# A hybrid decoder layer on one core: the input projection by seven block products a pair of column tiles instead of eight

## The chip, the cores and the metric

The kernel runs on one core of one Trainium2 chip. The metric is the device time of one execution in microseconds, the median of several runs. The engines are named as in the profile: PE is TensorE (matrix multiplication), PEld its weight loads, DVE is VectorE, ACT is ScalarE, POOL is GpSimd, and SP is the engine that issues almost all DMA transfers. Each engine works through its own list of instructions strictly in order. Where an instruction has to wait for a semaphore, everything behind it on that engine waits too.

## The reference

One layer of a causal decoder over 1024 tokens of width 1024, all in float32:

```
xn   = rms_norm(x, norm1_w)
proj = xn @ w_in            # 1024 x 6408: q, k, v (768 each), conv q/k/v (1536), beta and a (8), z (512), 2 gates (1024 each)
o_a  = three groups of 4 heads, causal windows (128,1), (512,4), (2048,16), softmax, combined by their log-denominators
o_b  = gated delta rule in chunks of 64 on silu(conv(dqkv)), 4 heads of 128, rms_norm, times silu(z)
y    = sigmoid(gate_a) * (o_a @ w_pa) + sigmoid(gate_b) * (o_b @ w_pb)
h    = x + y @ w_o
out  = rms_norm(h + (silu(conv gate) * conv val) @ w_down, final_norm_w)   # conv(rms_norm(h) @ w_up), d_ff 2816
```

To keep float32 accuracy, the kernel writes every operand of a matrix product as a high part (rounded to the type fp32r) and a low part (the rest), and adds three products: high by high, high by low and low by high.

## The kernel before, in words

**Stages.** A head normalises x, transposes it and splits it into `xh` and `xl` (8 tiles of K by 1024 tokens each). The mixer computes the input projection and, between its matmuls, the delta rule and attention. `merge_and_project` computes the branch projections, the gates and the output projection. `ffn` follows. Its up projection already uses seven block products in place of eight (class `UpRoom`).

**The input projection before.** It is 51 jobs: one of 16 columns (`ba`), then 50 of 128 columns: 12 `conv`, 4 `z`, 18 `q`, `k`, `v` and 16 `gate`. A job of 128 columns is 8 steps of K, and each step (an item `mm`, which calls `product3`) is 6 matmuls 128x512: three products by two halves of the tokens. So a job is 48 matmuls into one of the two accumulators `acc`. Its weights arrive as one 512 KB load (`w_raw`). ACT makes the high part (L1085) and POOL the low part (L1007). At the end of the job ACT empties the accumulator (`evac`).

**What sets the order.** `mixer_schedule` writes one list of items by hand. Every engine's function (`x_sync`, `x_gpsimd`, `x_scalar`, `x_vector`, `x_tensor`) walks the same list and emits its own part of each item, so the list is the order of all queues. A slot is one step of K. Between the slots stand the stages of the delta rule (items `dn`, 162 of them) and of attention. Attention is 24 units of 128 queries, eight for each of three groups. Each unit is `a_qk` (scores on PE, L1505; mask, maximum on DVE, L1382 to L1386; four exponentials on ACT, L1179), `a_pT` (transposes on PE, L1516; copy on ACT) and `a_pv` (values on PE, L1523; copy on DVE, L1393). `a_pT` can't start before the last exponential. The list leaves 3, 2 and 1 slots behind these three. In 11 of the 24 units a query block sees 256 keys, in the others 128. Behind the last unit come eight steps that combine the three groups (`cmbA`, `cmb`, `cmbT`), DVE work for the most part.

**Where results go before.** q, k and v stay in SBUF (`qk`, `vt`, `V`). The gates and seven of the eight chunks of the delta rule's output pass through DRAM.

## Time and profile before

| What | Value |
|---|---|
| Median of 3 runs | 1611.21 us (1611.08 to 1611.26) |
| Profiled execution, span from first to last instruction | 1610.9 us |
| PE busy | 1583.4 us (98%) |
| DVE, POOL, ACT busy | 885.1, 641.8, 580.8 us |
| Matmuls | 7913 |

Only the span of the profiled execution is recorded. It is 0.3 us shorter than the median, so what lies around the span is within 0.3 us, and a sum made against the span stands 0.3 us below the median. Busy time of an engine is the time in which at least one of its instructions runs. Matmuls overlap, so their mean durations can't be added: the distance from the start of one to the start of the next is what counts.

### The profile page before, as it was taken

The page shows a single profiled execution, that of the slowest core. Times are in us where ns is not written, and L with a number is a line of the kernel's source. Part 1 is how long each engine was busy: PE and PEld are TensorE (multiplying, and loading weights), DVE is VectorE, ACT ScalarE, POOL GpSimd, SP SyncE. Part 2 cuts the span into 40 slices and gives each one's busy share as a digit, 9 for nine tenths or more (in the row PEclk, how much of TensorE's full clock was granted, in tenths as well). Part 3 has the DMA queues.
Part 4 walks back from the last instruction along what each step waited for, and adds up shares of the span by engine and source line. Part 5 has one row for each costly group of instructions (what it writes and reads, how often), then busy time and mean ns, then how long its engine had stood idle before and what let it go on. Part 6 is the DMA issues. An engine that isn't in the chain of part 4 may idle for free.

```text
span 1610.9 us, 20471 instructions
## 1 busy us (share of the span) xinstructions
PE 1583.4 (98%) x7913; PEld 1321.1 (82%) x7913; DVE 885.1 (55%) x1326; ACT 580.8 (36%) x857; POOL 641.8 (40%) x471
## 2 busy tenths in 40 slices
PE   6999999999999999999999999999999999999998
PEld 4888888888888888888788887888888888878886
DVE  5232321454535353566554148756666566788886
ACT  4422222132322254333222134444444444444445
POOL 3333422312121223224324347987778888100111
PEclk9999999999999999999999999999999999999999
DMA  5222352221313142445457031432233432697685
GB/s 173 66 79 84 100 159 65 54 70 52 79 42 88 34 138 45 133 128 152 137 205 261 14 114 33 135 92 92 92 98 113 123 118 84 232 314 234 199 263 183
DMA packets 206444, 196.47 MB, mean 122 GB/s; under 512 B 23524, under 2 KB 157196, under 8 KB 206348
## 3 DMA queue, kind: packets, MB, share of 16 engines
q1 hardware_dynamic: 206128, 195.08, 39.2%
q8 instruction: 63, 1.03, 0.3%
q14 instruction: 33, 0.27, 0.1%
q10 hardware_dynamic: 220, 0.09, 0.0%
HBM read 146.76 MB, written 48.37 MB: 121 GB/s over the span
## 4 chain that ended last, share of the span: by engine, by line
PE 92%; DVE 5%; DMA 2%; issue 1%; ACT 1%; SPq 0%; POOL 0%; DVEq 0%; ACTq 0%
PE acc L566 37%; PE acc L2507 12%; PE bank_ab L1442 7%; PE bank_ab L2507 7%; PE acc L2517 6%; PE att_ps L2507 5%; PE bank_ab L2517 3%; PE acc L1877 3%; PE att_ps L2517 3%; PE att_ps L1523 2%; PE bank_ab L1877 1%; PE att_ps L1877 1%; PE att_ps L1505 1%; DMA f_raw<-in_w_down_dram 1%; DVE u_t_full L1833 1%; PE att_ps L1516 1%
## 5 line engine op out<-in xcount | busy, mean ns | idle before, releaser
L566 PE MATMUL acc<-xh,w_high 128*128 128x512 f32 x832 | 274.0, 406 | 0.6 <-POOL xl L1766 0.6
L566 PE MATMUL acc<-xl,w_high 128*128 128x512 f32 x832 | 262.3, 392 | 0.0
L1007 POOL TENSOR_TENSOR w_low<-w_raw,w_high 128x1024 fp32r<-128x1024 f32 x49 | 117.4, 2395 | 363.1 <-ACT w_high L1085 363.1
L566 PE MATMUL acc<-xh,w_low 128*128 128x512 f32 x832 | 261.3, 390 | 0.0
L566 PEld LDWEIGHTS acc<-xh,w_low 128*128 128x128 f32 x832 | 156.6, 188 | 34.3
L566 PEld LDWEIGHTS acc<-xl,w_high 128*128 128x128 f32 x832 | 156.5, 188 | 33.8
L566 PEld LDWEIGHTS acc<-xh,w_high 128*128 128x128 f32 x832 | 146.9, 189 | 23.9 <-POOL xl L1766 1.0
L1179 ACT ACTIVATE sc<-sc,mx 128x128 f32<-128x128 f32 (+1 forms) x96 | 35.5, 441 | 172.3 <-DVE mx L1386 172.3
L1279 DVE SCALAR_TENSOR_TENSOR cs<-acc,prm,cs 128x1023 f32<-128x1023 f32 (+2 forms) x36 | 46.1, 1282 | 79.5 <-ACT cs L1103 78.6
L2283 POOL TENSOR_TENSOR f_h<-f_h,f_fw 128x512 f32<-128x512 f32 x8 | 11.0, 1369 | 170.5 <-ACT f_junk L2206 170.5
L2517 PE MATMUL acc<-f_w_high,f_gh 128*128 128x512 f32 x176 | 68.8, 391 | 0.0
L2517 PE MATMUL acc<-f_w_low,f_gh 128*128 128x512 f32 x176 | 68.5, 389 | 0.0
L2517 PE MATMUL acc<-f_w_high,f_gl 128*128 128x512 f32 x176 | 68.5, 389 | 0.0
L375 POOL TENSOR_TENSOR u_own<-u_s,u_own 128x512 fp32r<-128x512 f32 x42 | 66.0, 1590 | 0.0
L2198 ACT ACTIVATE f_w_high<-f_raw 128x512 fp32r<-128x512 f32 x55 | 34.8, 633 | 79.8 <-DMA f_raw<-in_w_down_dram 19.4
L375 POOL TENSOR_TENSOR w_low<-u_s,w_high 128x512 fp32r<-128x512 f32 x42 | 54.5, 1298 | 8.4 <-ACT w_high L371 8.4
L2300 DVE SCALAR_TENSOR_TENSOR u_conv<-acc,prm,u_conv 128x1023 f32<-128x1023 f32 (+1 forms) x44 | 55.4, 1279 | 0.8
L371 ACT ACTIVATE u_own<-u_s 128x512 fp32r<-128x512 f32 x42 | 26.4, 632 | 80.6 <-POOL u_s L358 68.2
L2372 DVE TENSOR_TENSOR f_gl<-f_raw,f_gh 128x512 fp32r<-128x512 f32 x77 | 53.9, 700 | 0.0
L2326 DVE TENSOR_TENSOR acc<-u_free_low,acc 128x512 f32<-128x512 f32 x40 | 27.8, 694 | 45.7 <-PE acc L2507 45.7
L1393 DVE COPY O<-att_ps 128x260 f32<-128x260 f32 x24 | 10.3, 429 | 76.0 <-PE att_ps L1523 75.9
L1085 ACT ACTIVATE w_high<-w_raw 128x1024 fp32r<-128x1024 f32 x49 | 51.4, 1048 | 0.3 <-DMA w_raw<-in_w_in_dram 0.3
(391 smaller groups left out, 3807.8 us busy)
## 6 DMA issues: line engine op xcount, KB each, us to landing
w_raw<-in_w_in_dram SPq DMA_DIRECT2D x51, 512.0 KB, 4.6
f_raw<-glu_d SPq DMA_DIRECT2D x66, 256.0 KB, 3.1
f_raw<-in_w_down_dram SPq DMA_DIRECT2D x55, 256.0 KB, 4.2
w_raw<-in_w_up_dram SPq DMA_DIRECT2D x24, 512.0 KB, 5.1
glu_d<-u_free_high SPq DMA_DIRECT2D x22, 512.0 KB, 4.6
u_raw_even<-in_w_up_dram SPq DMA_DIRECT2D x20, 512.0 KB, 4.7
f_raw<-gsum_d SPq DMA_DIRECT2D x33, 256.0 KB, 3.6
conv_d<-so SPq DMA_DIRECT2D x16, 512.0 KB, 3.0
```

The lines of the kernel that those rows point to most:

```text
L375: nc.gpsimd.tensor_tensor(self.vl[q], self.source(t, q), self.vh[q].bitcast(F32), ALU.subtract).then_inc(self.s_vlo, 1)
L566: mm = nc.tensor.matmul(out[:, lo:hi], w, xx[:, lo:hi], start=first and j == 0, stop=last and j == 2)
L1007: g.tensor_tensor(wl[:, n % 2], raw[:, n % 2], wh[:, n % 2].bitcast(F32), ALU.subtract).then_inc(s_wlo, 1)
L1085: g.activation(wh[:, n % 2], raw[:, n % 2], ACT.Copy).then_inc(s_whi, 1)
L1179: last = g.activation(sc[:, q, 0:nk], sc[:, q, 0:nk], ACT.Exp, bias=mx[:, 1, q:q + 1], scale=ATT_SCALE)
L1279: ins = g.scalar_tensor_tensor(c0[:, j:S], a[:, 0:S - j], prm[:, w:w + 1], c0[:, j:S], ALU.mult, ALU.add)
L1442: last = t_.matmul(out4[:, h, :], lhs[:, h, :], r, start=True, stop=True)
L1877: mm = nc.tensor.matmul(every[st], a[:, k, rows], b[k], start=first and j == 0, stop=last and j == 2)
L2300: ins = nc.vector.scalar_tensor_tensor(cv[:, j, tap:S], banks(t)[j][:, 0:S - tap], prm[:, w:w + 1], cv[:, j, tap:S], ALU.mult, ALU.add)
L2372: nc.vector.tensor_tensor(to, src, high.bitcast(F32), ALU.subtract).then_inc(s_low, 1)
L2507: mm = nc.tensor.matmul(to, w[:, k, :], x[:, k, :], start=k == 0 and j == 0, stop=k == KT // 2 - 1 and j == 2)
L2517: mm = nc.tensor.matmul(row_banks(p)[i], x[:, rows], w, start=kk == 0 and j == 0, stop=kk == KH - 1 and j == 2)
```

## The change

The first three jobs (`ba` and two `conv`) stay as they are. The other 48 are taken in 24 pairs. Call the pair's weights, by halves of K, a00 and a01 (second job) and a10 and a11 (first job), and the blocks of `x` (half of K by half of the tokens) b00, b01, b10 and b11. In place of eight block products a pair has seven, each of 4 steps of K by 3 matmuls 128x512:

```
s1 = a10+a11   s2 = s1-a00   s3 = a00-a10   s4 = a01-s2          (POOL, per pair)
t1 = b01-b00   t2 = b11-t1   t3 = b11-b01   t4 = b10-t2          (once, ahead of pair 0)
product 0: a00*b00   1: s2*t2   2: s3*t3   3: s1*t1   4: a11*t4   5: a01*b10   6: s4*b11
```

Between the products the results are combined in PSUM. `one` copies product 0 (ACT). `two` adds product 1 (DVE). `three` adds `two` to product 2 (DVE) and copies the sum (ACT). `four` makes two more sums (DVE). Products 4, 5 and 6 then accumulate on top: PE starts product 4 only after the copy of `three`, and product 6 only after the first sum of `four`. Each of the seven weight blocks is split into high (ACT) and low (POOL) parts in a ring of 3 places, so the split of product n+2 is in the list one step behind the start of product n.

A slot is now 3 matmuls. The gaps behind `a_qk`, `a_pT` and `a_pv` are 5, 4 and 2 slots, and a delta rule stage comes every 3 slots or beside an attention item. The groups of attention run in the order 2, 1, 0, and the combine steps of group 0 stand between its own units instead of behind the last one. q, k, v and 14 of the 16 gates pass through one staging tile of SBUF to DRAM, each unit loads its q, k and v again (`aload`), and both branch outputs pass through DRAM (`o_d`). POOL's masks move from the head into pairs 0 to 4. The square of the conv output moves from POOL to ACT.

The core of the diff:

```diff
+GROUP_ORDER = (2, 1, 0)
+PLAIN = 3
+NP = 7
+HK = KT // 2
+RING = 3
+TURN = NP * HK
+ATT_GAP = {"a_v": 3, "a_qk": 5, "a_pT": 4, "a_pv": 2}
+DN_GAP, DN_LONG = 3, 6
...
-    GAP = {"a_qk": 3, "a_pT": 2, "a_pv": 1}
-    for n, (kind, t, _) in enumerate(jobs):
-        for k in range(KT):
-            items.append(("mm", n, k))
+    for p in range(pairs):
+        for i in range(NP):
+            for k in range(HK):
+                slot = p * TURN + i * HK + k
+                items.append(("mp", p, i, k))
...
+                if key == (3, 0):
+                    items.append(("three", p))
+                if key == (3, 1):
+                    items += [("split", p, 5), ("raw", p + 1, 3)]
...
+                if key == (4, 1):
+                    items += [("split", p, 6), ("raw", p + 1, 1)]
+                    if p + 1 < pairs:
+                        items += [("sum", p + 1, 1), ("sum", p + 1, 2)]
...
+                        if name == "a_pv" and u[0] == 0:
+                            c = u[1]
+                            for d, step in ((3, ("cload", c)), (9, ("cmbA", c)), (12, ("cmb", c)), (17, ("cmbT", c))):
+                                at_slot.setdefault(slot + d, []).append(step)
```

PE's part of one product:

```diff
+                if kind == "mp":
+                    p, i, k = it[1:]
+                    x, y = acc[1 - y_acc(p)], acc[y_acc(p)]
+                    n = NP * p + i
+                    if k == 0:
+                        pe.wait_ge(s_vlo, n + 1)
+                        if i == 0:
+                            pe.wait_ge(s_taken, pair_jobs(p)[0] - 1)
+                        if i == 2:
+                            pe.wait_ge(s_taken, pair_jobs(p)[0])
+                        if p == 0 and i in t_needed:
+                            pe.wait_ge(s_tlo, t_needed[i])
+                        if i == 4:
+                            pe.wait_ge(s_one, 2 * p + 2)
+                        if i == 5:
+                            pe.wait_ge(s_one, 2 * p + 1)
+                        if i == 6:
+                            pe.wait_ge(s_mix, 4 * p + 3)
+                    to = [x[:, first_cols], x[:, rest_cols], y[:, first_cols], y[:, rest_cols],
+                          y[:, first_cols], x[:, first_cols], x[:, rest_cols]][i]
+                    high, low = moving[i]
+                    for j, (w, xx) in enumerate(((vh[n % RING], high), (vh[n % RING], low), (vl[n % RING], high))):
+                        mm = t_.matmul(to, w[:, k, :], xx[:, k, :], start=i < 4 and k == 0 and j == 0,
+                                       stop=k == HK - 1 and j == 2, skip_group_check=True)
```

The sums on DVE and the split on ACT and POOL:

```diff
+                if kind == "three":
+                    dve.wait_ge(s_prod, NP * p + 3)
+                    dve.wait_ge(s_mix, 4 * p + 1)
+                    g.tensor_tensor(y[:, first_cols], two, y[:, first_cols], ALU.add).then_inc(s_mix, 1)
...
+                if kind == "three":
+                    act.wait_ge(s_mix, 4 * p + 2)
+                    g.activation(one, acc[y_acc(p)][:, first_cols], ACT.Copy).then_inc(s_one, 1)
...
+                if kind == "split":
+                    n = NP * it[1] + it[2]
+                    pool.wait_ge(s_vhi, n + 1)
+                    g.tensor_tensor(vl[n % RING], source[it[2]], vh[n % RING].bitcast(F32),
+                                    ALU.subtract).then_inc(s_vlo, 1)
```

**Order on PE, one 256-key unit.** This is PE's list inside attention, before: `L1505` are the scores, `L1442` delta rule stages, `L566` the projection (each row two matmuls), `L1516` the transposes.

```order
L1505 MATMUL att_ps<-qk 128x256 x4
L1442 MATMUL bank_ab<-d_S,ckqk 128x128 x8
L566 MATMUL acc<-xh,w_high 128x512 x2
L566 MATMUL acc<-xl,w_high 128x512 x2
L566 MATMUL acc<-xh,w_low 128x512 x2
...
L1516 MATMUL att_ps<-ident,sc 128x128 x8
```

The same place after, in group 0: `L1844` are the scores, `L1745` the delta rule, `L1796` the projection (each row one matmul), `L1872` the transposes of a combine step, `L1854` the transposes of the unit.

```order
L1844 MATMUL att_ps<-a_k_114,a_q_112 128x256 x4
L1745 MATMUL bank_ab<-d_S,ckqk_97 128x128 x8
L1796 MATMUL acc<-xh,w_high 128x512
L1796 MATMUL acc<-xl,w_high 128x512
L1796 MATMUL acc<-xh,w_low 128x512
...
L1872 MATMUL att_ps<-ident,a_ocb 128x128 x2
L1796 MATMUL acc<-xh,w_high 128x512
L1796 MATMUL acc<-xl,w_high 128x512
L1796 MATMUL acc<-xh,w_low 128x512
L1854 MATMUL att_ps<-ident,a_sc 128x128 x8
```

Between scores and transposes stood 18 matmuls 128x512; now there are 15.

**Order on DVE, the combine.** This is DVE's list behind attention, before: a whole combine step (`L1410` to `L1425`) stands between delta rule stages (`L1340`, `L1345`).

```order
L1340 TENSOR_TENSOR d_WT<-bank_ab,d_DTr 128x512
L1410 TENSOR_TENSOR cbs<-cbs,qk 128x12
L1411 TENSOR_TENSOR cbm<-cbs 128x4
L1412 TENSOR_TENSOR cbm<-cbm,cbs 128x4
L1413 RECIPROCAL cbm<-cbm 128x4
L1414 TENSOR_TENSOR cbs<-cbs,cbm 128x12
L1417 TENSOR_TENSOR qk<-qk,cbs 128x4x64 x3
L1424 TENSOR_TENSOR PT<-qk 128x256
L1425 TENSOR_TENSOR PT<-PT,qk 128x256
L1429 TENSOR_TENSOR g_ol<-att_ps,g_oh 128x2x128
L1345 TENSOR_TENSOR d_P<-bank_ab,lmask 128x512
```

After, inside group 0: the same step (`L1714` to `L1729`) is followed by the mask and the maximum of the next unit's scores (`L1685`, `L1688`, `L1689`).

```order
L1714 TENSOR_TENSOR cbs<-cbs,a_cb 128x12
L1715 TENSOR_TENSOR cbm<-cbs 128x4
L1716 TENSOR_TENSOR cbm<-cbm,cbs 128x4
L1717 RECIPROCAL cbm<-cbm 128x4
L1718 TENSOR_TENSOR cbs<-cbs,cbm 128x12
L1721 TENSOR_TENSOR a_cb<-a_cb,cbs 128x4x64 x3
L1728 TENSOR_TENSOR a_ocb<-a_cb 128x256
L1729 TENSOR_TENSOR a_ocb<-a_ocb,a_cb 128x256
L1685 TENSOR_TENSOR a_sc<-att_ps,amask 128x1024
L1688 TENSOR_REDUCE mx<-a_sc 128x4
L1689 TENSOR_SCALAR mx<-mx 128x4
```

The combine of unit c now stands directly ahead of the scores of unit c+2 on DVE, six times in all.

## Rows read from the trace of the kernel before

**Rows 1.** Page, busy time, share of the span and instructions of each engine.
```profile
PE 1583.4 (98%) x7913; PEld 1321.1 (82%) x7913; DVE 885.1 (55%) x1326; ACT 580.8 (36%) x857; POOL 641.8 (40%) x471
```

**Rows 2.** All waits: engine, line, releaser: total us, times, longest.
```profile
PE bank_ab L1442 <- DVE ckz L1369: 2.3, 1, 2.3
```

**Rows 3.** Timeline of ACT, 150 to 260 us: start, duration, instruction [idle before].
```profile
186.79 1.12 ACT L1103 ACTIVATE cs<-acc,prm 128x1024 f32<-128x1024 f32 x1 [4.04 <-PE acc L566]
...
197.67 1.03 ACT L1109 ACTIVATE so<-acc 128x1024 f32<-128x1024 f32 x1 [4.72 <-PE acc L566]
```

**Rows 4.** Timeline of the FFN's up projection, DVE, 1205 to 1226 us.
```profile
1213.36 0.69 DVE L2326 TENSOR_TENSOR u_free_low<-u_free_low,acc 128x512 f32<-128x512 f32 x1 [2.03 <-PE acc L2507]
...
1216.08 0.70 DVE L2326 TENSOR_TENSOR acc<-u_free_low,acc 128x512 f32<-128x512 f32 x1 [0.60 <-PE acc L2507]
```

**Rows 5.** Tile w_raw on POOL: duration ns min/median/max, first and last start.
```profile
L1007 POOL TENSOR_TENSOR w_low<-w_raw,w_high x49: 2344/2391/2558, 43.3 to 780.5; 128x1024 fp32r<-128x1024 f32 x49
L375 POOL TENSOR_TENSOR w_low<-w_raw,w_high x22: 1281/1302/3348, 999.4 to 1377.8; 128x512 fp32r<-128x512 f32 x22
...
L358 POOL TENSOR_TENSOR u_s<-u_s,w_raw x11: 1296/2152/2158, 971.4 to 1361.3; 128x512 f32<-128x512 f32 x11
```

**Rows 6.** Page, costliest groups: count, busy us, mean ns, idle before.
```profile
L566 PE MATMUL acc<-xl,w_high 128*128 128x512 f32 x832 | 262.3, 392 | 0.0
...
L371 ACT ACTIVATE u_own<-u_s 128x512 fp32r<-128x512 f32 x42 | 26.4, 632 | 80.6 <-POOL u_s L358 68.2
...
L2326 DVE TENSOR_TENSOR acc<-u_free_low,acc 128x512 f32<-128x512 f32 x40 | 27.8, 694 | 45.7 <-PE acc L2507 45.7
```

**Rows 7.** Stretches: us, busy PE, PEld, DVE, ACT, POOL; clock, DMA, GB/s.
```profile
320.00:400.00 80.00, 79.97 (x495) 67.64 (x494) 39.40 (x74) 22.14 (x38) 18.88 (x15) 1.00 0.24 61
1120.00:1200.00 80.00, 80.00 (x354) 66.25 (x353) 48.05 (x55) 33.57 (x46) 64.56 (x47) 1.00 0.32 99
```

**Rows 8.** Timeline around one 256-key attention unit, 342 to 372 us.
```profile
350.20 2.37 POOL L1007 TENSOR_TENSOR w_low<-w_raw,w_high 128x1024 fp32r<-128x1024 f32 x1 [14.31 <-ACT w_high L1085]
350.28 2.31 DVE L1395 COPY O<-mx 128x4 f32<-128x4 f32 x1
...
352.10 1.14 PE L1505 MATMUL att_ps<-qk 64*128 64x256 f32 x8
...
353.24 2.05 PE L1442 MATMUL bank_ab<-d_S,ckqk 128*128 128x128 f32 x16
...
354.87 1.23 DVE L1382 TENSOR_TENSOR sc<-att_ps,amask 128x1024 f32<-128x1024 f32 x1
...
357.59 1.71 ACT L1179 ACTIVATE sc<-sc,mx 128x256 f32<-128x256 f32 x4 [7.47 <-DVE mx L1386]
...
359.45 1.07 PE L1516 MATMUL att_ps<-ident,sc 128*128 128x128 f32 x8
...
360.35 1.06 PE L1442 MATMUL bank_ab<-d_U,d_P 128*128 128x128 f32 x8
```

**Rows 9.** DVE groups by form, 60 to 800 us: the combine's first and last.
```profile
L1417 DVE TENSOR_TENSOR qk<-qk,cbs 128x256 f32<-128x256 f32 x24 | 16.1, 725 | 0.3
...
L1412 DVE TENSOR_TENSOR cbm<-cbm,cbs 128x4 f32<-128x4 f32 x8 | 1.3, 162 | 0.3
```

**Rows 10.** Page, DMA issues: KB each, us from issue to landing.
```profile
f_raw<-in_w_down_dram SPq DMA_DIRECT2D x55, 256.0 KB, 4.2
...
g_gates<-gate_d SPq DMA_DIRECT2D x8, 1024.0 KB, 5.5
```

**Rows 11.** Stretches around one long wait, columns as in rows 7.
```profile
994.00:996.00 2.00, 0.01 (x1) 0.00 (x0) 2.00 (x1) 2.00 (x2) 0.00 (x0) 1.00 1.08 322
...
998.00:1000.00 2.00, 2.00 (x7) 1.52 (x6) 2.00 (x2) 2.00 (x3) 2.00 (x2) 0.50 0.00 0
```

**Rows 12.** Timeline, 35 to 37 us: the head's last write of xl.
```profile
35.81 1.22 DVE L492 TENSOR_TENSOR xl<-bank_ab,xh 128x1024 fp32r<-128x1024 f32 x1 [2.04 <-ACT xh L445]
```

979 lines of the change are left out of this document (618 added, 361 removed).

## The prediction

> **What bounds the kernel now.** I read the page first. PE is busy for 1583.4 of 1610.9 us [rows 1], so it sets the end almost everywhere, and only fewer or shorter PE intervals can bring much. The list of waits says how little PE stands still: in the whole mixer the one wait over 2 us is 2.3 us [rows 2]. The mean of a matmul, 392 ns [rows 6], is its latency and not its cost, because the next one starts long before it ends. The cost I take from two emptyings of the accumulator that lie one pure job apart: ACT starts them at 186.79 and 197.67 us [rows 3]. That is 10.88 us for 48 matmuls, or 226.7 ns each. The reader is to see this trap: with 390 ns the change would look worth 112 us. The FFN, which already works with seven products, gives the same pitch in that order of matmuls: DVE takes two products at 1213.36 and 1216.08 us [rows 4], 2.72 us for 12 matmuls.
>
> The other engines have room on average. Inside attention PE is busy 79.97 of 80 us, DVE 39.40, ACT 22.14 and POOL 18.88 [rows 7]. But each engine works strictly in order, and that is where a shorter PE path can open waits.
>
> **What the change removes.** Before, 48 jobs of 48 matmuls make 2304. After, 24 pairs of 7 x 4 x 3 = 84 make 2016. The 288 that go, at 226.7 ns, are 65.3 us. Attention, the delta rule and the transposes of v keep their matmuls (six jobs of eight transposes before, 24 units of two after). So with no new wait the span would be 1610.9 - 65.3 = 1545.6 us. A pair then takes 19.04 us of matmuls instead of 21.76.
>
> The Trainium skill, TensorE: Matmul & The Clock Gate, section "Wait — 56ns, not 53.3ns?", gives N/2.4 GHz plus 2.5 ns from start to start. By the page, an estimate for 512 columns is 215.7 ns and a saving of 62.1 us. The rows show 226.7 ns, and the measured pitch decides.
>
> **What it adds beside PE.** Splits: seven weight blocks a pair, each 0.63 us on ACT [rows 6] and 1.30 us on POOL [rows 5]. The four sums of weights are POOL operations of the same shape, 1.30 us at best and 2.15 us at the median of one kind of them [rows 5]. POOL: 11 x 1.30 = 14.3 us a pair in place of 2 x 2.39 = 4.8. In the FFN's stretch POOL works 64.56 of 80 us beside a full PE [rows 7], so the load is bearable. ACT: 7 x 0.63 + 2 x 0.63 = 5.7 us in place of 2 x 1.05. DVE: 4 x 0.69 = 2.8 us [rows 6], new. None of this is on the path while it is on time, and I cost it at nothing by itself. Its cover is the lead of the lists. A split (0.63 + 1.30 and two hops of 0.2, 2.3 us) has 7 slots of 0.68 us = 4.8 us before PE needs it. `three` (0.69 on DVE, 0.63 on ACT, three hops: 1.9 us) has one product, 2.72 us. So PE has 0.8 us of slack there, 24 times. Before, a split had most of a job, 10.88 us.
>
> The extra DMA (18 tiles of 512 KB out, 24 units in) stands beside PE too. DMA is used by 0.24 in attention [rows 7]. A block of weights of 256 KB should land like the FFN's, in 4.2 us [rows 10].
>
> **Rows against the skill, on the shared port.** Row first: DVE's copy of 128x4 elements took 2.31 us, from 350.28 to 352.59, while POOL's `w_low` ran from 350.20 to 352.57 [rows 8]. POOL blocked it for its whole length. The Trainium skill, SBUF — State Buffer, section "SBUF: two separate sides", says that the pair is an exclusive lock for a whole instruction, also against DVE operations with two SBUF inputs. By that rule, the trace agrees. What it does here, from rows: POOL's operations get half as long (1.30 us for 2.39) and more than twice as many, so what is caught waits half as long, but twice as often or a little more. I see no gain or loss in that. The new sums on DVE read one operand from PSUM and showed 0.69 us in the FFN beside a POOL at 80% [rows 6, 7], so I charge them nothing.
>
> **The waits it adds, one by one.**
>
> 1. *The transposes of a long unit in attention.* Before, PE's scores ended at 353.24 and its transposes began at 359.45 [rows 8]. The mask began at 354.87 because DVE was late by 1.6 us, the exponentials ran from 357.59 to 359.30. PE was filled by a delta rule stage of 2.05 us and 18 matmuls, 4.08 us. It was just enough. Now 15 matmuls take 3.40 us. From the end of the scores the chain takes 2.72 (mask to first exponential) + 1.71 + 0.15 = 4.6 us when DVE is free and 6.1 us as in the rows. PE has 3.40 plus a stage of 1.06 or 2.05: 4.5 to 5.5 us. The wait is 0 to 1.6 us. I take 0.8 for five of the 11 long units: 4 us. The short ones have half the work and no wait.
> 2. *The same in group 0, behind the combine.* In six units DVE's `cmb` step now stands directly ahead of the mask. The combine is 12 groups of operations, from 16.1 us to 1.3 us, together 48.8 us for eight steps [rows 9], 4.7 us of each step in `cmb`. It starts 1.8 us before the scores end (a slot of 0.68 and the scores' 1.14), so the mask begins 2.9 us late: 2.9 + 4.6 = 7.5 us against 4.8 to 5.8 that PE has (two transposes of the combine add 0.3, at 1.07 us for eight, rows 8). The wait is 1.7 to 2.7 us, six times. I take 2.0: 12 us.
> 3. *`three` and the splits behind a blocked engine.* In the 15 pairs in which the delta rule or attention runs, ACT waits for DVE's maximum in each unit, and DVE waits for the stages. The block lasts 6.1 us [rows 8], against 0.8 us slack of `three` and 2.5 us of a split. But PE also gets attention and delta rule work of its own in that time, about 1 us an item, and most units don't stand right before a `three`. The lower bound is 0, the upper 15 x 2.5 = 37 us. I take 0.6 a pair: 9 us, near the lower end, because the FFN shows the same chain without a wait beside a DVE at 60%.
> 4. *The head.* t1 to t3 and the splits of t1 to t4 are about seven DVE passes of 128x2048. One pass of 128x1024 is 1.22 us, and DVE is free for it from 37.03 us [rows 12], so they are 17 us of DVE beside 20 us of plain jobs and the first products. 0 to 6 us: I take 2.
> 5. *The tail of the mixer.* 3 MB of branch outputs are loaded from the middle of pair 22, and ACT waits for all of it at the start of pair 23, 14 slots or 9.5 us later. At 5.5 us for 1 MB [rows 10] it may take 16.5 us, which blocks ACT for 7 us, against 6.8 us that product 3 can spare and 2.6 us of split and copy. 0 to 4 us: I take 2.
>
> The sum of the waits is 4 + 12 + 9 + 2 + 2 = 29 us. 1545.6 + 29 = 1574.6 us of span, and 0.3 us more for the median: 1575.
>
> On the clock: after 2 us in which PE did nothing (994 to 996 us) the granted clock was 0.50, the level of 1.2 GHz, from 998 to 1000 us [rows 11], which costs 1 us of work in those 2. The other long waits are few in the rows, so how often a wait brings that can't be read from them. I charge nothing and let the range hold up to 10 us for it.
>
> **Rivals.**
>
> *A, the forecast (0.58).* 1575, own range 1560 to 1592.
>
> *B, all waits hidden (0.22).* For it: the FFN runs its seven products at a full PE for 80 of 80 us [rows 7]. Against it: the FFN has no attention and no solving chain on DVE. Only the six waits behind the combine would be left at half size: 1545.6 + 6 = 1552.
>
> *C, POOL's sums at the pair's edge bind (0.11).* The last weight block is asked for at the start of product 3, one slot in, and lands 4.2 us later [rows 10], 2.2 us into product 4. From there to the low part that product 2 of the next pair needs, POOL has four sums and three splits. At 1.30 us each they are done at 11.3 us, and PE begins that product at 5 x 2.72 = 13.6. At 2.15 us for the sums [rows 5] it is 14.7, 1.1 us too late, and with a load that lands 1 us later 2.1. 1.6 us x 24 = 38 us with half of terms 1 to 3: 1545.6 + 38 + 12 = 1596. For it: the slow kind of sum. Against it: the same sums in the FFN.
>
> *D, slower (0.09).* ACT is the one engine that must serve softmax, `three` and every split. If its block by the softmax (6.1 us from scores to last exponential, rows 8) always falls onto a product with 2.5 us to spare, PE loses 3.6 us in each of 24 units: 86 us, above the 65.3 saved. With term 5 that is 1545.6 + 86 + 2 = 1634. It decides as soon as a pair loses more than 65.3 / 24 = 2.72 us, which is one whole product. Against it: PE's own work in that time, as above.
>
> **How the numbers follow.** The time is A's. C and D lie above, B below. The range 1551 to 1604 takes in A, B's centre and C's lower part, and leaves out about 0.17. Within 0.2% (3.2 us) this kernel can't be told from no change. Faster by more than that: A, B, and most of C, 0.89 with a little from D. I say 0.88, the same 0.03, slower 0.09.
>
> **What would show it.** Right: 2016 matmuls 128x512 in the pairs, 19.0 us from pair to pair where no other stage stands between (pairs 22 to 23), PE waits for the last exponential under 1 us in groups 2 and 1 and near 2 us in group 0 with DVE's combine ahead of the mask, and PE's waits in total near 29 us above before. Wrong: waits of PE for POOL's `w_low` at the start of products 0 to 2 in every pair (C), waits for ACT's `m_one` or `w_high` of 3 us and more in most units (D), or an unbroken PE in group 0 (B). The forecast as a whole fails if the pitch of the pairs' matmuls isn't 227 ns.

## The result: slower by 3%, where 2% faster was forecast

| | Before | After |
|---|---|---|
| Median | 1611.14 us (1611.01 to 1611.26) | 1658.88 us (1656.37 to 1663.19) |
| Span of the profiled execution | 1610.9 us | 1654.6 us |
| Granted clock, mean over the span | 0.997 | 0.978 |

The ratio is 1.0301, 95% interval 1.0286 to 1.0315. The time lies 84 us above the forecast of 1575 and far outside its range. The span of the profiled execution of after is 4.3 us shorter than the median, so what follows explains 43.7 of the 47.7 us.

The page after, busy time of each engine, answers to [rows 1]:

```profile
PE 1554.6 (94%) x7625; PEld 1280.4 (77%) x7625; DVE 971.3 (59%) x1421; ACT 676.6 (41%) x1059; POOL 863.1 (52%) x675
```

The 288 matmuls are gone (7913 - 7625). But PE's idle time (span less busy) went from 27.5 to 100.0 us, and its busy time fell by only 28.8 us in place of 65.3. The saving itself is real. ACT's copy of product 0, once a pair, on ACT's timeline of after (start, duration, instruction):

```profile
92.24 0.58 ACT L1342 ACTIVATE m_one<-acc 128x512 f32<-128x512 f32 x1
...
115.18 0.58 ACT L1342 ACTIVATE m_one<-acc 128x512 f32<-128x512 f32 x1
...
138.16 0.58 ACT L1342 ACTIVATE m_one<-acc 128x512 f32<-128x512 f32 x1
```

A pair takes 22.96 us, in the mean of two. In it stand two batches of 16 small matmuls for the norms. PE's timeline:

```profile
94.01 1.84 PE L1804 MATMUL bank_ab<-ones,sqb 128*128 128x1 f32 x16
```

84 x 0.2267 + 2 x 1.84 = 22.72 us, so a pair is within 0.24 us of the forecast. The pitch itself is a little longer. Over all pairs, wherever one projection matmul follows another without a break, the mean distance from start to start is 230.8 ns, against 228.1 ns before. Over 2016 matmuls that is 5.4 us.

Where PE stands still, by stretches of after (us, busy PE, PEld, DVE, ACT, POOL, clock, DMA, GB/s):

```profile
0.00:80.00 80.00, 64.73 (x307) 49.29 (x308) 55.40 (x51) 51.66 (x65) 39.78 (x42) 0.98 0.37 114
80.00:160.00 80.00, 80.00 (x398) 66.75 (x396) 36.77 (x36) 39.21 (x52) 56.51 (x56) 1.00 0.29 89
160.00:240.00 80.00, 56.61 (x228) 44.45 (x227) 27.65 (x43) 25.22 (x39) 49.09 (x40) 0.86 0.38 105
240.00:600.00 360.00, 342.28 (x2022) 290.56 (x2022) 192.60 (x358) 129.68 (x252) 195.93 (x163) 0.97 0.41 117
600.00:800.00 200.00, 171.49 (x997) 144.69 (x995) 123.13 (x267) 80.94 (x134) 84.59 (x71) 0.94 0.40 116
```

The same stretches of before:

```profile
0.00:80.00 80.00, 67.80 (x321) 52.59 (x322) 32.51 (x44) 38.48 (x51) 26.67 (x55) 0.98 0.39 120
...
160.00:240.00 80.00, 80.00 (x360) 65.98 (x359) 23.46 (x33) 21.37 (x24) 29.66 (x13) 1.00 0.46 133
240.00:600.00 360.00, 358.56 (x2156) 306.69 (x2155) 163.14 (x312) 99.73 (x162) 82.90 (x57) 1.00 0.26 67
600.00:800.00 200.00, 197.37 (x1138) 168.36 (x1137) 118.24 (x265) 67.71 (x104) 63.54 (x46) 1.00 0.41 114
```

Line by line, idle after less idle before: 3.1 us in the head, 0 while plain pairs run, 23.4 from 160 to 240 us, 16.3 from 240 to 600, 25.9 from 600 to 800. The remaining 3.9 us come from 800 us on. From 80 to 160 us PE is full, so the seven products alone run without a hole, though POOL is at 71%, the highest load of these five stretches. In the three stretches from 160 to 800 us, where PE waits, no other engine is busy for more than 62%.

PE's waits in after, the longest in total, by engine, line and releaser (us in total, times, longest), answer to [rows 2]:

```profile
PE att_ps L1854 <- ACT a_ocb L1469: 20.1, 6, 6.3
PE acc L1796 <- POOL w_low L1241: 16.1, 6, 9.9
...
PE acc L1796 <- ACT m_one L1346: 9.7, 1, 9.7
PE bank_ab L1745 <- DVE d_P L1653: 9.0, 3, 4.5
PE att_ps L1844 <- DVE O L1697: 7.1, 3, 3.2
PE att_ps L1872 <- DVE a_sc L1685: 5.3, 3, 2.2
```

Three places explain most of these lines.

**A power operation on POOL.** POOL takes the norms of the conv outputs, 128x64 elements to the power -0.5. The timeline:

```profile
157.42 10.56 POOL L1246 TENSOR_TENSOR rr<-rr,hp 128x64 f32<-128x64 f32 x1 [0.76 <-DVE rr L1596]
...
160.90 0.62 ACT L1335 ACTIVATE w_high<-m_sum 128x512 fp32r<-128x512 f32 x1
...
168.91 1.27 POOL L1241 TENSOR_TENSOR w_low<-m_sum,w_high 128x512 fp32r<-128x512 f32 x1
170.23 0.80 PE L1796 MATMUL acc<-m_t_high,w_high 128*128 128x512 f32 x1 [9.86 <-POOL w_low L1241]
```

The high part was ready at 161.5, but its low part stood behind the power. Before, the same operation took 10.57 us (start 158.84) beside a POOL that owed PE nothing for most of a job of 10.88 us. Now POOL owes PE a low part every 2.72 us.

**A trip through DRAM on DVE's path.** To solve its triangular systems, the delta rule stores a block (eight transfers) and loads it back with another layout. DVE's timeline, chunk 0:

```profile
231.22 0.16 DVE L1513 COPY sol<-m 32x2 f32<-32x2 f32 x1 [11.66 <-DMA m<-m_d]
...
234.30 0.69 DVE L1564 TENSOR_TENSOR m_two<-m_one,acc 128x512 f32<-128x512 f32 x1
235.09 0.69 DVE L1570 TENSOR_TENSOR acc<-m_two,acc 128x512 f32<-128x512 f32 x1
235.69 0.69 DVE L1573 TENSOR_TENSOR acc<-m_two,acc 128x512 f32<-128x512 f32 x1
235.82 0.60 ACT L1346 ACTIVATE m_one<-acc 128x512 f32<-128x512 f32 x1 [13.78 <-DVE acc L1570]
...
236.56 0.76 PE L1796 MATMUL acc<-xh,w_high 128*128 128x512 f32 x1 [9.66 <-ACT m_one L1346]
```

The waiting copy takes 0.16 us, but `two`, `three` and `four` stand behind it. DVE stood still for 11.66 us, and PE for 9.66.

**Group 0 of attention with the combine inside.** One unit at 675 us, all engines:

```profile
675.57 1.14 PE L1844 MATMUL att_ps<-a_k,a_q 64*128 64x256 f32 x8
...
675.96 1.01 DVE L1716 TENSOR_TENSOR cbm<-cbm,cbs 128x4 f32<-128x4 f32 x1
...
681.28 1.22 DVE L1685 TENSOR_TENSOR a_sc<-att_ps,amask 128x1024 f32<-128x1024 f32 x1
...
683.99 1.70 ACT L1454 ACTIVATE a_sc<-a_sc,mx 128x256 f32<-128x256 f32 x4 [10.01 <-DVE mx L1689]
685.60 1.26 ACT L1434 ACTIVATE d_DTr<-d_DTr,g_all 128x128 f32<-128x128 f32 x4
686.87 1.28 ACT L1385 ACT_TABLE_LOAD   x1
...
688.17 1.02 ACT L1385 ACTIVATE staging<-acc 128x1024 f32<-128x1024 f32 x1
...
689.09 0.62 ACT L1335 ACTIVATE w_high<-w_raw 128x512 fp32r<-128x512 f32 x1
689.61 0.38 ACT L1469 ACTIVATE a_ocb<-att_ps 128x256 f32<-128x256 f32 x1
...
690.03 0.69 PE L1854 MATMUL att_ps<-ident,a_sc 128*128 128x128 f32 x2 [6.35 <-ACT a_ocb L1469]
```

The mask starts 4.6 us after the scores end, against 1.6 us in [rows 8]. The last exponential is done at 685.69, but PE's transposes come 4.3 us later. PE's previous use of the same bank, the combine's two transposes, must first be copied by ACT, and that copy stands behind a decay of the delta rule, a table load, an evacuation and a split.

**The clock.** Around the long wait of 9.86 us (columns as in the stretches above):

```profile
168.00:170.00 2.00, 0.00 (x0) 0.00 (x0) 1.88 (x5) 0.00 (x0) 1.75 (x4) 0.50 0.00 0
170.00:172.00 2.00, 1.77 (x4) 1.49 (x5) 1.96 (x2) 0.00 (x0) 1.86 (x3) 0.50 0.00 0
172.00:174.00 2.00, 2.00 (x7) 1.53 (x7) 0.54 (x1) 1.06 (x1) 2.00 (x2) 0.62 0.07 13
174.00:176.00 2.00, 2.00 (x10) 1.61 (x9) 0.69 (x1) 0.63 (x1) 0.50 (x2) 1.00 0.98 321
```

The clock is at its lower level (0.50, 1.2 GHz) while PE waits and for about 3 us after it works again. Around the wait of 9.66 us it stands at 0.50 from 231.6 to 241.8 us, and PE works for 5.2 of these. In all the clock is at 0.50 for 71.4 us of the span, against 9.2 before. PE is busy in 46.0 of them, against 6.8 before; the rest falls into waits and costs nothing. At half speed this is, as an estimate, 23.0 us of work lost against 3.4, so 19.6 us more.

**The account.** Saved 65.3; idle time 72.5 more; busy time that didn't fall 36.5. That makes +43.7. Of the 36.5, 19.6 are the estimate for the clock, 5.4 the longer pitch in the pairs, and 8.0 slower matmuls behind the projection (the last experiment below). 3.5 us are left open.

### The profile page after: what moved, and what is told of

Read it like the earlier page. It is cut to its first block, busy times and chain, and to the rows that moved or that the text cites. A ratio compares the mean times of both kernels' runs of the same rounds, so it can differ in the third digit from the quotient of the medians.

```text
span 1654.6 us, 21066 instructions
## 1 busy us (share of the span) xinstructions
PE 1554.6 (94%) x7625; PEld 1280.4 (77%) x7625; DVE 971.3 (59%) x1421; ACT 676.6 (41%) x1059; POOL 863.1 (52%) x675
## 4 chain that ended last, share of the span: by engine, by line
PE 74%; DVE 10%; POOL 4%; DMA 4%; SPq 3%; ACT 3%; issue 2%; DVEq 0%; ACTq 0%; POOLq 0%
PE acc L1796 17%; PE acc L2852 12%; PE acc L2862 7%; PE bank_ab L2852 7%; PE att_ps L2852 5%; PE acc L672 5%; PE bank_ab L1745 5%; PE bank_ab L2862 3%; PE att_ps L2862 3%; PE acc L2221 3%; DMA m<-m_d 2%; DVE prod L1517 1%; PE bank_ab L2221 1%; PE att_ps L2221 1%; PE att_ps L1862 1%
## 5 line engine op out<-in xcount | busy, mean ns | idle before, releaser
L1241 POOL TENSOR_TENSOR w_low<-w_raw,w_high 128x512 fp32r<-128x512 f32 x96 | 126.1, 1314 | 173.0 <-ACT w_high L1335 172.7
L1796 PE MATMUL acc<-xh,w_high 128*128 128x512 f32 x384 | 160.4, 418 | 12.4 <-ACT m_one L1346 9.7
L1796 PE MATMUL acc<-xl,w_high 128*128 128x512 f32 x384 | 152.9, 398 | 0.0
L1796 PE MATMUL acc<-xh,w_low 128*128 128x512 f32 x384 | 152.7, 398 | 0.0
L1241 POOL TENSOR_TENSOR w_low<-m_sum,w_high 128x512 fp32r<-128x512 f32 x72 | 98.2, 1364 | 97.8 <-ACT w_high L1335 97.8
L1796 PE MATMUL acc<-m_t_high,w_high 128*128 128x512 f32 x288 | 120.5, 418 | 13.4 <-POOL w_low L1241 13.3
L1796 PE MATMUL acc<-m_t_high,w_low 128*128 128x512 f32 x288 | 114.7, 398 | 0.0
L1796 PE MATMUL acc<-m_t_low,w_high 128*128 128x512 f32 x288 | 114.5, 397 | 0.0
L1796 PEld LDWEIGHTS acc<-xh,w_high 128*128 128x128 f32 x384 | 74.5, 194 | 28.5 <-issue 11.6
L1796 PEld LDWEIGHTS acc<-xh,w_low 128*128 128x128 f32 x384 | 73.8, 192 | 16.7
L1796 PEld LDWEIGHTS acc<-xl,w_high 128*128 128x128 f32 x384 | 74.4, 194 | 13.3
L1796 PEld LDWEIGHTS acc<-m_t_high,w_high 128*128 128x128 f32 x288 | 55.1, 191 | 25.7 <-POOL w_low L1241 15.6
L1796 PEld LDWEIGHTS acc<-m_t_high,w_low 128*128 128x128 f32 x288 | 54.7, 190 | 13.0
```

What stands on the lines that cost most here:

```text
L1241: g.tensor_tensor(vl[n % RING], source[it[2]], vh[n % RING].bitcast(F32), ALU.subtract).then_inc(s_vlo, 1)
L1796: mm = t_.matmul(to, w[:, k, :], xx[:, k, :], start=i < 4 and k == 0 and j == 0, stop=k == HK - 1 and j == 2, skip_group_check=True)
```

## The experiments

Each is a change to the changed kernel ("after", 1658.9 us) and is timed against the kernel before (1610.4 to 1612.0 in each set). A gain between sets is good to about 3 us. The theory throughout: PE waits because instructions that it needs stand behind others in an in-order queue. The rival: POOL, DVE or ACT is full there, so that a change of order only moves the wait.

### The power operation: e1 and e5

In e1 the power is cut into eight pieces, spread over the slots:

```diff
-                    items += {(5, 2): [("rnorm",)]}.get(key, [])
+                    items += {(5, 2): [("rnorm",), ("rpow", 0)], (5, 3): [("rpow", 1)], (6, 2): [("rpow", 2)],
+                              (6, 3): [("rpow", 3)]}.get(key, [])
```

> The changed kernel (1658.9 us) with POOL's power operation over 128x64 values (10.56 us in its trace) cut into eight pieces of 8 columns, which stand one by one between the weight splits, and what reads the result moved behind the last piece. Theory 1, blocked queue: PE's wait of 9.86 us for POOL's w_low at 170 us was the length of this one operation, and the clock at half for some 3.5 us behind it cost 1.7 more. The wait goes, the time falls by 9 to 13 us, to 1646 to 1650. Rival: the splits are late there because POOL has too much work in any case (56.5 of 80 us busy just before). Then the pieces, which together are longer than the whole (about 13 us), leave the wait in small parts and the time stays at 1656 to 1660.

Measured: 1660.3 us, ratio 1.0303 (1.0286 to 1.0321), no gain. The wait of 9.86 us became four of 1.4 to 2.8 us. POOL's timeline of e1:

```profile
163.22 3.27 POOL L1252 TENSOR_TENSOR rr<-rr,hp 128x8 f32<-128x8 f32 x2 [0.77 <-DVE rr L1603]
```

A piece of 128x8 takes 1.63 us and comes on top of the low parts and sums POOL owes there. The forecast of 1646 to 1650 missed, and the result lies at the upper edge of the rival's 1656 to 1660. In e5 the power is left out, a constant stands in its place:

```diff
-                    g.tensor_tensor(flat, flat, hp64[:], ALU.pow).then_inc(s_rr, 1)
+                    g.tensor_scalar(flat, flat, 0.0, 0.02, ALU.mult, ALU.add).then_inc(s_rr, 1)
```

> The changed kernel (1658.9 us) in which POOL's power operation of 10.56 us is replaced by one that sets a constant (about 0.3 us), so the lengths of q and k are left out of the result. Cutting it into pieces gained nothing (1660.3 us): four waits of 8.1 us in total came in place of one of 9.9. Theory now: POOL has no room there at all, so only less work helps, and the whole 10 us on POOL are on PE's path with 1.7 us of clock. The time falls by 9 to 13 us, to 1646 to 1650, and no wait for w_low is left at 160 to 185 us. Rival: POOL catches up whatever it is given, and the limit is the next one in the list (the loads on SP at 205 us, the solving step at 230 us), so the gain is under 4 us.

Measured: 1647.7 us, 1.0218 (1.0201 to 1.0235), within the forecast of 1646 to 1650: the power costs 11.2 us. The theory had no wait for `w_low` left from 160 to 185 us. In the whole run there are seven, all short now:

```profile
PE acc L1796 <- POOL w_low L1241: 8.1, 7, 2.4
```

### The returned block: e2, e4 and e7

In e2 the block is stored and loaded as before, into other rows of the tile, but DVE solves with zeros and doesn't wait:

```diff
-                    dve.wait_ge(s_ml, 16 * (c + 1))
```

> The changed kernel in which DVE's solving step reads a block of zeros set at the start instead of the block that came back from DRAM. The store and the load are still issued and land beside it, so only DVE's wait for them is left out, and the delta rule's output is not the right one. Theory 1: DVE stood still for 18.8 us in five such waits (11.66 us the longest), and because two, three and four of the block products stand behind it, PE waited 9.7 us for the copy of three, twice 4.4 us for d_P, and part of 7.1 us for the copy of O. The time falls by 18 to 30 us with the clock behind the waits, to 1629 to 1641. Rival: these PE waits come from the load of the weights that was late (SP's queue) or from POOL, and return elsewhere: less than 8 us gained, 1651 or more.

Measured: 1643.4 us, 1.0204 (1.0188 to 1.022), 2 us above the forecast of 1629 to 1641. The trip costs 15.5 us: that is chunk 0's wait of 9.7 and whatever hung on DVE's four other waits for a returned block. In its trace the wait for `m_one` is gone from the first rows. Those for `d_P` have gone from 9.0 to 5.1 us: the one at 286 us fell from 4.5 to 0.9 us, but the one of 4.3 us at 339 us is still 4.2 us long (at 329 us), so it doesn't hang on this trip.

e4 keeps the work and puts the first solving step of the later chunks one stage later:

```diff
-kkD + rest + [("P5", c)] + ml + [("T5", c)] + ob + sv0
-        out += [("P6", c)] + sv1 + [("kS", c)] + sv2 + ts
+kkD + rest + [("P5", c)] + ml + [("T5", c)] + ob
+        out += [("P6", c)] + sv0 + [("kS", c)] + sv1 + sv2 + ts
```

> The changed kernel with the first part of the solving step of chunks 1 to 7 one stage of the delta rule later (behind P6), and the second part beside the third. It gives the round trip through DRAM some 3 us more, in the right computation. Chunk 0 stays as it is. Theory 1: the two PE waits for d_P of 4.5 and 4.3 us and part of those for O go, and the longest wait (9.7 us, chunk 0) stays. Gain 6 to 12 us: 1647 to 1653. Rival: DVE's burst at the later stage (4 us in one piece) delays the sums of the block products, or the loads behind it on SP come late for the next chunk: no gain, 1656 to 1665.

Measured: 1659.0 us, 1.0296 (1.0274 to 1.0318), no gain, as the rival had it. The waits for `d_P` left the first rows of the list, and waits for the exponentials (6.0 us) and longer ones for the mask (7.0 us, against 5.3) came.

e7 puts two more empty stages ahead of chunk 0's solving and loads two of its inputs later:

```diff
-kkD + rest * 2 + ml + rest + sv0 + rest * 3
+kkD + rest * 2 + ml + rest * 3 + sv0 + rest * 3
```

> The changed kernel with two edits on the way to the first solution of the delta rule, in the right computation: three empty steps in place of one between the store of chunk 0's system and its solving step, and the loads of v and of chunk 1 moved from the first block of loads on SP to later items. Without any wait of DVE for the DRAM trip the time was 1643.4, 15.5 us less. Of its PE waits the longest, 9.7 us at 236 us, belongs to chunk 0. Theory: two steps of 2.0 us and the shorter SP queue take 5 to 9 us from that wait and 2 us from the one for ckqk and w_low at 205 to 214 us, and with the clock the time falls by 7 to 13 us: 1646 to 1652. Rival: SP's queue fills up behind the stores of the system, and the loads of the next weight block come late in their place: under 4 us.

Measured: 1671.9 us, 1.0371 (1.0355 to 1.0386), 13 us slower. Chunk 0's wait fell from 9.7 to 6.6 us, but the delta rule now meets group 0 six slots later. PE is busy there 158.87 of 200 us, in place of 171.49:

```profile
600.00:800.00 200.00, 158.87 (x892) 134.39 (x893) 118.03 (x249) 73.64 (x123) 73.46 (x61) 0.90 0.35 102
```

The theory was right on the one wait and useless for the sum. My explanation is that a list written by hand is one schedule, and moving one stage by six slots moves every later meeting. It is argued and not shown, but e16 below, which keeps the later places, fits it.

### The combine: e3, e6, e9 and e15

e3 moves the combine's steps later within the unit:

```diff
-((3, ("cload", c)), (9, ("cmbA", c)), (12, ("cmb", c)), (17, ("cmbT", c)))
+((9, ("cload", c)), (16, ("cmbA", c)), (19, ("cmb", c)), (23, ("cmbT", c)))
```

> The changed kernel with the combine steps of group 0 moved 7 slots later in the list (loaded at 9, first part at 16, main part at 19, transposes at 23 slots behind a_pv, in place of 3, 9, 12 and 17). So DVE's 4.7 us of combine stand behind the scores' maximum and not ahead of it, and the transposes of the combine stand between two units. My forecast's term 2: the combine ahead of the mask costs PE 12 us; the trace showed PE's waits inside group 0 (618 to 759 us) at 27.6 us, with 20.1 of them for the copy behind the exponentials. Theory: most of that goes, the time falls by 15 to 28 us with its share of the clock, to 1631 to 1644. Rival: DVE is simply too full in that stretch (51 of 80 us busy, the port shared with POOL stretches small operations from 0.16 to 1.0 us), so the wait only moves to other items: less than 8 us gained, 1651 or more.

Measured: 1655.9 us, 1.0281 (1.0257 to 1.0305), 3 us at best, where 15 to 28 had been forecast. `a_ocb` L1469 went, and in its place came waits for `O` (11.0 us new, and 8.6 us where there were 7.1) and for `a_ocb` L1729 (6.7 us).

e6 puts all eight steps behind the last unit, as the kernel before had them, 8 slots apart:

```diff
-                        if name == "a_pv" and u[0] == 0:
-                            c = u[1]
+                        if name == "a_pv" and u == units[-1]:
+                            for c in range(NT):
+                                for d, step in ((2, ("cload", c)), (7, ("cmbA", c)), (9, ("cmb", c)), (12, ("cmbT", c))):
+                                    at_slot.setdefault(slot + 8 * c + d, []).append(step)
```

> The changed kernel with this one part undone: the eight combine steps of group 0 stand behind the last attention unit, 8 slots apart, as they did before the change, and no longer between the units. Moving them by 7 slots within the units gained 3 us only, and DVE stayed 59.3 of 80 us busy there. Theory: DVE has too much work in that stretch for three concurrent chains, not a bad order, so taking 5.9 us a unit out of it (49 us in all) and giving them to the emptier pairs 20 to 22 removes most of the 27.6 us of PE's waits between 618 and 759 us. The time falls by 18 to 32 us, to 1627 to 1641. Rival: the waits belong to the schedule of attention itself (256 keys, gaps of 5 slots) and stay, gain under 8 us.

Measured: 1667.4 us, 1.0344 (1.0329 to 1.036), 8.5 us slower, where 18 to 32 us of gain had been forecast. Between 640 and 720 us PE is now busy 78.05 of 80 us, and the loss stands behind the last unit:

```profile
640.00:720.00 80.00, 78.05 (x491) 65.62 (x490) 43.42 (x80) 39.51 (x66) 35.49 (x30) 1.00 0.36 104
720.00:800.00 80.00, 60.95 (x298) 50.65 (x297) 53.43 (x119) 24.70 (x40) 33.19 (x30) 0.87 0.36 99
```

I took the eight waits there for a spacing fault: the transposes stood three slots (2.0 us) behind a DVE step of 4.7 us. e9 gives them six slots:

```diff
-(9, ("cmb", c)), (12, ("cmbT", c))
+(9, ("cmb", c)), (15, ("cmbT", c))
```

> The combine of the two head halves is put last as in e6, but its transposes stand six slots behind it instead of three; everything is computed as in the changed kernel. Theory (the waits come from VectorE's order: what TensorE needs stands behind the combine there): the eight waits for the combine's output copies of e6 (1.8 to 4.8 us each, about 25 us) go, and the time is 1632 to 1645 us. Rival (VectorE and GpSimd together are full in this stretch, the waits only change their place): other waits of the same sum come up, 1658 to 1668 us.

Measured: 1672.3 us, 1.0375 (1.0358 to 1.0392), 4.9 us above e6 and above the rival's range too. 8 slots are 5.4 us, and a combine with its preparation keeps DVE busy for 4.3 to 8.1 us there, 6.4 in the mean, so DVE falls behind whatever the distance. The waits became 6.2 us for `d_P`, 3.8 for `ckz` and 8.9 for the combine.

e15 leaves the combine in its place and cuts it into three pieces:

```diff
+(8, ("cmbA", c)), (10, ("cmbM", c)), (12, ("cmbX", c)), (13, ("cmb", c)), (17, ("cmbT", c))
```

> The changed kernel with VectorE's combine in three pieces, with one or two slots of other work between them, everything computed. Theory (its length in one piece of 5 to 6 us makes the waits in group 0): waits there fall from 27.6 to about 12 us, time 1635 to 1648 us. Rival (what counts is the sum of VectorE's and GpSimd's work in a unit's 7.5 us): 1655 to 1665 us.

Measured: 1662.3 us, 1.0312 (1.0292 to 1.0331), no gain, as the rival had it: cutting this work into pieces doesn't help while all of it stays on DVE.

### Taken together: e8, e10, e12, e13

e12 is e5 and e2 in one, with both diffs as above.

> Constant factors in place of the power operation, and the delta rule without the use of the returned block; the combine as in the changed kernel. If the two gains add (11.2 and 15.5 us): 1632 us. If one hid behind the other: 1640 to 1645 us; if they help each other: below 1627 us. It is the base for e13.

Measured: 1632.4 us, 1.0133 (1.0115 to 1.0152). The gains add: 26.5 us against 11.2 + 15.5 = 26.7.

e8 is e12 with e6's combine, e10 is e12 with e9's:

> The changed kernel without POOL's power operation (e5), without DVE's wait for the DRAM trip of the solving step (e2) and with the combine behind attention (e6), all three at once; its output is not the right one, as in e2 and e5. Theory: these three places hold most of PE's lost time of the changed kernel (100 us idle against 27.5 before, and 31 us more of half clock), and they are independent, so the gains add up: 15.5 + 11 + 25 = 51 us, and the time is 1600 to 1616, about the kernel before. Rival, capacity: what is taken away in one place returns at the next in-order queue, the three together gain less than 35 us, and the time stays above 1624. A third: the half clock behind long waits goes with them and the sum is larger than the parts, below 1600.

> Without the power operation (constant factors in place of the norms), without the use of the returned block in the delta rule, and with the combine last and spaced. Theory: the three kinds of wait make up nearly all of what was lost against the 65.3 us of matmuls saved; TensorE's idle time falls to 40 to 50 us, the granted clock rises to 0.99, time 1595 to 1610 us. Rival (time is bounded by the other engines' sum): 1620 to 1632 us, as in e8.

Measured: 1632.0 us, 1.0128 (1.0112 to 1.0143), and 1640.5 us, 1.0185 (1.017 to 1.02). Against e12, moving the combine gives nothing, and the wider spacing costs 8. My theories missed: 1600 to 1616 for e8, whose rival (above 1624) held, and 1595 to 1610 for e10, which lies above its rival's 1620 to 1632 as well.

e13 is e12 without the scaling in DVE's combine (`L1714` to `L1721` left out):

```diff
-                    link(g.tensor_tensor(cbs[:, 2], cbs[:, 1], X[:, :, :, DH], ALU.mult))
...
-                    for q in range(NG):
-                        ins = g.tensor_tensor(X[:, q, :, 0:DH], X[:, q, :, 0:DH],
```

> As e12, and VectorE's combine leaves out the scaling by the softmax sums (five small operations and three of 128x256): about 5 us of VectorE a chunk, 40 us in eight chunks. Theory (the combine stands in front of what TensorE waits for in group 0): most of the 27.6 us of waits and the lower clock behind them go, 20 to 30 us faster than e12, about 1605 us. Rival (the waits there come from the softmax's own chain of VectorE, ScalarE and TensorE): within 8 us of e12.

Measured: 1610.8 us, 0.9996 (0.9987 to 1.0005): 21.6 us less than e12, and level with the kernel before. The stretch in e12 (columns as above):

```profile
600.00:800.00 200.00, 172.71 (x962) 144.97 (x963) 112.00 (x232) 81.85 (x134) 97.14 (x80) 0.94 0.38 115
```

and in e13:

```profile
600.00:800.00 200.00, 186.68 (x1022) 156.45 (x1021) 97.77 (x172) 85.18 (x135) 102.08 (x82) 0.97 0.39 118
```

PE works 14.0 us more in the same 200. Over the whole span DVE's busy time falls from 979.4 to 956.4 us, by 23.0, and the time by 21.6. So the time falls by about as much as DVE's work, though DVE is busy for only 56% of the stretch in e12. e3, e6, e9 and e15 moved or cut this work and gained 3 us or nothing; only taking it away helped. What e13 doesn't tell apart is DVE's load and the time until the combine's result is there: it takes away both.

### How much was cover: e14

The 288 matmuls come back: in three of the seven products the matmul of `w_high` and the low part of x is issued twice.

```diff
-                    for j, (w, xx) in enumerate(((vh[n % RING], high), (vh[n % RING], low), (vl[n % RING], high))):
+                    for j, (w, xx) in enumerate(((vh[n % RING], high), (vh[n % RING], low), (vl[n % RING], high),
+                                                 (vh[n % RING], low))[:4 if i in (1, 3, 5) else 3]):
```

> The changed kernel with 288 added matmuls of 128x512, 12 in each pair (the second product of three of the seven blocks is summed twice, so the output isn't the reference's): as much TensorE work as before the change. Theory (the matmuls covered the other engines' queues): the waits and the clock's loss go back to the size of before, so the time is 1650 to 1675 us, nearly that of the changed kernel. Rival (the waits are there whatever the cover): 65 us more, 1715 to 1725 us.

Measured: 1696.2 us, 1.0516 (1.0491 to 1.054), 37.3 us above after: between the two forecasts. So of 65.3 us of matmuls, 28.0 took the place of what is lost otherwise, and 37.3 did not. PE's idle time went from 100.0 to 79.9 us. The cover theory holds for less than half. Chunk 0's wait stays at 9.5 us and the one behind the power at 9.1:

```profile
PE acc L1797 <- POOL w_low L1241: 11.4, 3, 9.1
...
PE acc L1797 <- ACT m_one L1346: 9.5, 1, 9.5
```

These two are chains, not lack of cover: with as many matmuls as before the change they are nearly as long.

### Versions that compute everything: e11, e16, e17

e16 takes the power by ACT, starts the delta rule six slots earlier and has e7's two edits (one load earlier still), so that chunk 0 gets the lead of e7 and the later chunks keep their places:

```diff
-DN_FROM = 5 * TURN + 2 * HK
+DN_FROM = 5 * TURN + 2 * HK - 6
...
-                    g.tensor_tensor(flat, flat, hp64[:], ALU.pow).then_inc(s_rr, 1)
+                    g.activation(flat, flat, ACT.Ln).then_inc(s_lnr, 1)
+                    act.wait_ge(s_lnr, 1)
+                    g.activation(flat, flat, ACT.Exp, scale=-0.5).then_inc(s_rr, 1)
```

e11 is the same with e9's combine.

> A version that computes everything: the norms' power is taken by ScalarE (logarithm and exponential) in place of GpSimd, the delta rule starts six slots earlier on chunk 0, and the combine stands last and spaced. Theory: the wait of 9.9 us and the wait of 9.7 us shrink to 1 to 3 us each, and the combine's waits go: 1608 to 1625 us, about as the kernel before. Rival (the earlier delta rule and ScalarE's added work only move the waits): 1630 to 1650 us.

> The norms' power by ScalarE (logarithm and exponential) and the delta rule's first chunk six slots earlier, the combine as in the changed kernel; everything is computed. e11 against e9 gained 22.8 us with these two, so by the theory 1634 to 1640 us; by the rival (in the changed order of the combine the earlier delta rule meets attention, as in e7) 1645 to 1660 us.

Measured: e11 1649.5 us, 1.0245 (1.0221 to 1.027), 22.8 less than e9 but in its rival's range and 24.5 above its own. e16 1642.1 us, 1.0186 (1.0171 to 1.0202), 16.8 less than after and between its two forecasts. The wait for POOL's `w_low` fell from 16.1 to 6.9 us and chunk 0's from 9.7 to 4.3. PE from 160 to 240 us is busy 72.12 us in place of 56.61:

```profile
160.00:240.00 80.00, 72.12 (x322) 57.65 (x321) 33.09 (x49) 33.07 (x50) 55.76 (x48) 0.98 0.45 135
```

e17 adds to e16 that ACT scales the combine's inputs:

```diff
-                    for q in range(NG):
-                        ins = g.tensor_tensor(X[:, q, :, 0:DH], X[:, q, :, 0:DH], ...
+                    for q in range(NG):
+                        for h in range(AH):
+                            ins = g.activation(X[:, q, h, 0:DH], X[:, q, h, 0:DH], ACT.Copy, scale=cbs[:, 3, q, h:h + 1])
```

> As e16, and the combine's three multiplications of 128x256 go from VectorE to ScalarE as twelve of 128x64 with a factor per row. Theory (VectorE's and GpSimd's sum is what delays group 0): waits there shrink by a third to a half, 8 to 15 us faster than e16. Rival (ScalarE's queue, with the attention's exponentials and the evacuation behind, is as tight): no gain or up to 10 us slower.

Measured: 1640.7 us, 1.0198 (1.0173 to 1.0223), level with e16, as the rival had it. From 600 to 800 us DVE works 5.4 us less (111.52 to 106.15) and ACT 26.7 us more (75.71 to 102.38). The waits for `a_ocb` fell by 5.3 us and those for `O` rose by 5.1. Taking work off DVE alone is therefore not enough where another queue of the same chain gets it. No version tried beats the kernel before.

### Where the tiles lie: e18

One remainder had no wait. Behind the projection PE has the same 3518 matmuls, and yet the branch sums to the last matmul take 807.2 us (839.2 to 1646.4) against 797.5 (805.1 to 1602.6). Of these 9.7 us PE is busy for 8.0 more (801.75 against 793.72) and idle for 1.7 more. Duration in ns (min/median/max) and first and last start of the matmuls that stream `g_oh`, before:

```profile
L566 PE MATMUL acc<-g_oh,w_high x96: 389/389/389, 805.1 to 869.3; 128*128 128x512 f32 x96
```

and after, for the same tile, and then for two kinds of matmul of the FFN's up projection. Both stream `xh`, which hasn't moved; the first has its weights in `u_own`, which has, and the second in `w_high`, which hasn't:

```profile
L672 PE MATMUL acc<-g_oh,w_high x84: 392/395/398, 847.6 to 905.3; 128*128 128x512 f32 x84
```

```profile
L2852 PE MATMUL bank_ab<-xh,u_own x88: 390/392/404, 1026.7 to 1418.8; 128*128 128x512 f32 x88
L2852 PE MATMUL bank_ab<-xh,w_high x88: 389/389/504, 1041.1 to 1432.1; 128*128 128x512 f32 x88
```

So it isn't the streamed tile alone that counts, but the place of the weights too. From start to start the slow ones are 233 ns in place of 226.7 (for the FFN's, 233.0 with `u_own` and 226.8 with `w_high`): on PE's timeline two start in 0.47 us (870.02, 870.49, 870.95) instead of 0.45 (840.06, 840.51, 840.96). The tile `g_oh` moved from byte 183456 of a partition to 183840. The remainder to 256 bytes changed from 160 to 32. e18 moves every tile behind the third row tile by 128 bytes:

```diff
-ROWS_AT = (BASE_AT, BASE_AT + 4096, BASE_AT + 8192, BASE_AT + 13440, BASE_AT + 17536, BASE_AT + 21632, BASE_AT + 25728,
-           BASE_AT + 116096)
+ROWS_AT = (BASE_AT, BASE_AT + 4096, BASE_AT + 8192, BASE_AT + 13568, BASE_AT + 17664, BASE_AT + 21760, BASE_AT + 25856,
+           BASE_AT + 116224)
```

> The changed kernel with all tiles behind the third row tile 128 bytes further on (remainder to 256 bytes 160 in place of 32, as in the kernel before); order and work are the same. Theory (a matmul that streams from such a place is 2 to 3% slower): g_oh matmuls back to 389 ns, the stages from the branch sums to the last matmul 797 to 799 us in place of 807, and with the blocks' 864 matmuls 10 to 15 us in all: 1644 to 1649 us. Rival (the 395 ns have another cause, such as the neighbouring instructions): 393 to 395 ns stay, time 1656 to 1661 us.

Measured: 1651.0 us, 1.0239 (1.0221 to 1.0257), 7.9 us faster than after. The same tile in e18:

```profile
L672 PE MATMUL acc<-g_oh,w_high x84: 389/389/389, 849.6 to 905.6; 128*128 128x512 f32 x84
```

Behind the projection all moved tiles are back at 389 ns, and these stages take 798.5 us (841.5 to 1640.0). The gain is 2 us short of the expected 10. In the projection e18 gave back only a part. Product 1, whose block was moved, went from 232.1 to 228.3 ns from start to start, and product 3, also moved, from 232.5 to 229.9. Product 2 stayed (232.7 and 232.9): its block starts at byte 384, remainder 128, and wasn't moved. These are means from start to start where no other stage stands between.

## Why the prediction was wrong, point by point

**The removal, 65.3 us: right but for 5 us.** The count of 288 holds, and the warning against 390 ns too. The pitch held before, but in the pairs it is 230.8 ns, in part by the addresses of two blocks (229.7 in e18). From product 1 of pair 22 (800.82 us) to that of pair 23 (820.66) PE takes 19.84 us, with 0.4 of the delta rule in it, where 19.0 was the sign to look for.

**"None of this is on the path while it is on time, and I cost it at nothing by itself": this step failed first.** I checked the mean load of POOL, DVE and ACT and the lead of a split (4.8 us) and of `three` (0.8 us), but not the longest single thing that stands in each queue. Two were longer than any lead of the lists. POOL's power operation of 10.56 us is in the trace of before at 158.84 us and in no term of the sum; it costs 11.2 us. DVE's wait for the returned block was in no term either; it costs 15.5 us. From 160 to 240 us 23.4 us of idle time arose where I had forecast none. Term 3's block of 6.1 us was taken from attention, and the longest blocks lay in the delta rule.

**Term 1 and term 3 (4 + 9 us): 16.3 us from 240 to 600 us.** The sum is near by luck, since neither mechanism is in the trace. In groups 2 and 1 PE never waits for the exponentials (term 1), nor for `three` while attention runs, and for a split for 0.7 us once (term 3). What stands there are 9.0 us of waits for `d_P` behind the solving and 7.1 us of scores that wait for DVE's copy `O`. Of the two long waits for `d_P`, e2 takes one away with the DRAM trip; the cause of the other (4.3 us) stays open.

**Term 2 (12 us): 25.9 us from 600 to 800 us, twice the size.** The place and the cause were right: DVE's combine ahead of the mask, six units. What I mis-sized was not DVE's step: in the unit shown it took 5.8 us (675.56 to 681.35), but that is the longest of eight, and their mean is 4.1 where I had 4.7. I let PE go on at the last exponential, while the transposes also wait for ACT's copy of the combine, which stands behind 4 us of other ACT work in the unit shown. All six of these waits (20.1 us) end with that copy, and three more (5.3 us) of the combine's own transposes wait for the mask. Without the combine's scaling the whole gains 21.6 us.

**Terms 4 and 5 (2 + 2 us): 3.1 us in the head and 3.9 from 800 us on.** Right in size, but by other waits than I named. In the head PE waits 2.4 us for ACT's square, ahead of which ACT made two of the block tiles (1.9 us each) and waited 1.3 us for DVE. In the tail it waits 3.2 us for POOL's `w_low`, and ACT's wait for the branch outputs is 0.6 us.

**The clock, 0 with up to 10 in the range: 19.6 us by the estimate above.** I had one wait of 2 us as a sample. Behind the long waits it stayed at 0.50 for 3.3 and 5.2 us of PE's work, which by the same estimate adds 1.6 us to the wait of 9.86 us and 2.6 to that of 9.66. So the clock adds to the cost of every other error.

**Not thought of: addresses.** I read the diff of the layout as free. Moving the tiles back in e18 gains 7.9 us.

**The rivals.** D had the right sign, though its 1634 us lies 25 below the result, and ACT was its engine; in the trace ACT's queue is only one of three, in one stage. C named POOL but at every pair's edge, where nothing shows: from 80 to 160 us PE is full. B is excluded. What I should have priced is a rival that no single engine holds: each of three in-order queues must give PE something within 2.72 us, and all three carry work with waits of its own.

**What stays open.** Saved and lost together, 109 us went: 65.3 and 43.7. Shown by experiment are 11.2, 15.5, 21.6 and 7.9, that is 56 us. For the rest look at e13, which is level with the kernel before and so still loses the 65.3 us it saves. There 34.9 us are idle time against before (62.4 less 27.5), in many small waits: behind the head PE's longest is 4.7 us. 9.5 us of it are PE's waits for ACT's `a_ocb` in group 0, which stay without the scaling. About 11 us are the clock, by the same estimate, and about 13 the slower matmuls (8.0 and 5.4), most of which e18 shows. I haven't taken these small waits apart, and their cause stays open. Nor was e18 combined with e16. Were the gains to add as those of e5 and e2 do, that would be about 1634 us.

## What to carry to other kernels

When matmuls go away, don't ask whether the other engines have room on average: list, for each in-order queue that PE waits on, the longest instruction and the longest foreign wait in it, and compare these with the new lead. A long wait costs more than its length, since the clock stays low behind it. A wait that is only moved in a hand-written list came back elsewhere here: e1, e3, e4, e6, e7, e9 and e15 gained 3 us at best and lost up to 13. Taking work or a wait away gained 11 to 22 us, but handing it to another queue of the same chain (e17) gained nothing. And after any change of layout compare the matmul durations of the untouched stages first.

## What the hardware showed that I had not expected

- The start address of a matmul's tiles changes its pitch: 226.7 ns and 389 ns duration where the start leaves a remainder of 160 bytes when divided by 256, and 233 ns and 392 to 395 ns where it leaves 32, and back again in e18. It holds for the streamed tile (`g_oh`) and for the tile of the weights (`u_own`). One block at a remainder of 128 is slow as well (232.7 ns), but was never moved. In the down projection, whose weights `f_gh` and `f_gl` were moved too, the effect is smaller: 228.9 ns, against 227.1 before and 226.9 in e18. Other places were not tried. Whether the start itself counts or the distance to other tiles isn't shown. All have 4-byte operands and 512 columns.
- POOL's power is slow, and grows with the elements in a partition: 10.56 us for 64, 1.63 us for 8, against 0.24 us for a multiply and add of the same 64 (e5).
- A DVE operation of 128x4 took 1.01 us at 675.96 beside POOL's `d_o_on` (1.04 us), against a mean of 0.16 us for the same operation before [rows 9]. The Trainium skill, SBUF — State Buffer, section "SBUF: two separate sides", has the pair of DVE and POOL as an exclusive lock for a whole instruction, and the trace agrees.
